# Three rounded products in place of one plain fp32 product for the attention output of the second block

## The reference, cut to what matters

```
def dsa_attention(q, k, v, qi, ki, wi, k_sel):          # block of 128 queries
    ...                                                  # the 128 best keys of each query are chosen
    s = jnp.einsum('bqgrd,bqkgd->bqgrk', qg, kg) * scale
    s = jnp.where(valid[:, :, None, None, :], s, -jnp.inf)
    p = jax.nn.softmax(s, axis=-1)
    o = jnp.einsum('bqgrk,bqkgd->bqgrd', p, vg)          # the product that is changed
```

## Time and profile before

| | us |
|---|---|
| median of three runs | 1981.89 |
| span of the profiled execution, first to last instruction | 1979.5 |
| TensorE busy, matrix products (PE) | 1954.4 |
| TensorE busy, loads of the stationary operand (PEld) | 1586.5 |
| VectorE busy (DVE) | 1212.9 |
| ScalarE busy (ACT) | 728.8 |
| GpSimd busy (POOL) | 875.7 |

### The profile page before, as it was taken

How to read it: one execution, slowest core, us unless ns; L and a number is a source line. 1 busy time by engine, 2 the same in 40 slices (tenths; PEclk the granted TensorE clock), 3 DMA queues, 4 the chain that set the end, 5 groups by cost and what they waited for, 6 DMA issues and landing times.

```text
span 1979.5 us, 23758 instructions
## 1 busy us (share of the span) xinstructions
PE 1954.4 (99%) x9127; PEld 1586.5 (80%) x9127; DVE 1212.9 (61%) x2188; ACT 728.8 (37%) x1057; POOL 875.7 (44%) x595
## 2 busy tenths in 40 slices
PE   8999999999999999999999999999999999999999
PEld 6777888888888766888888878888888888787787
DVE  3455442499999774222223588888888874795344
ACT  4345432232333344222223333333333334635452
POOL 1000000006878888887700677777787600720000
DMA  7543333146666667866657799999999923332122
GB/s 245 169 136 121 124 111 127 43 142 146 147 147 144 139 118 199 244 146 146 148 183 253 249 373 355 381 373 349 363 375 359 387 75 96 86 88 62 44 95 85
DMA packets 178592, 374.91 MB, mean 189 GB/s; under 512 B 56880, under 2 KB 92208, under 8 KB 169008
## 3 DMA queue, kind: packets, MB, share of 16 engines
q1 hardware_dynamic: 109264, 277.03, 41.0%
q0 software_dynamic: 64000, 84.12, 16.5%
q10 hardware_dynamic: 5216, 12.26, 1.7%
HBM read 312.38 MB, written 60.95 MB: 189 GB/s over the span
## 4 chain that ended last, share of the span: by engine, by line
PE 95%; DVE 3%; ACT 1%; issue 1%; DMA 0%; SPq 0%; DVEq 0%; ACTq 0%
PE bank L1558 35%; PE bank L329 18%; PE bank L331 17%; PE bank L330 17%; PE bank L1438 1%; PE bank L2237 1%; PE bank L1184 1%; PE bank L2217 1%; PE bank L548 1%; PE bank L2226 1%; PE bank L569 0%; DVE mix L919 0%; PE bank L419 0%; DVE v_low L1813 0%; PE bank L604 0%
## 5 line engine op out<-in xcount | busy, mean ns | idle before, releaser
L1412 POOL DMA_INDIRECT gates_scratch<-slot_gate,slot_place x256 | 441.5, 1725 | 299.4 <-DVE slot_place L1379 205.6
L1558 PE MATMUL bank<-xn_low,u_high 128*128 128x512 f32 x1024 | 410.3, 401 | 0.0
L1558 PE MATMUL bank<-xn_high,u_high 128*128 128x512 f32 x1024 | 399.9, 391 | 0.0
L1558 PE MATMUL bank<-xn_high,u_low 128*128 128x512 f32 x1024 | 398.6, 389 | 0.0
L1609 DVE TENSOR_TENSOR u_low<-u_raw,u_high 128x1024 fp32r<-128x1024 f32 x128 | 156.4, 1223 | 265.1 <-ACT u_high L1580 264.7
L329 PE MATMUL bank<-v_high,w_high 128*128 128x512 f32 x768 | 299.3, 390 | 1.4 <-DVE v_low L1813 1.4
L330 PE MATMUL bank<-v_low,w_high 128*128 128x512 f32 x768 | 299.1, 390 | 0.0
L331 PE MATMUL bank<-v_high,w_low 128*128 128x512 f32 x768 | 299.1, 389 | 0.0
L322 DVE TENSOR_TENSOR weights_low<-weights_raw,weights_high 128x1024 fp32r<-128x1024 f32 (+1 forms) x105 | 127.7, 1217 | 228.2 <-ACT weights_high L311 228.2
L1704 POOL DMA_INDIRECT row_unit<-units_scratch,slot_place x128 | 175.1, 1368 | 145.8 <-DMA units_scratch<-hidden 107.1
L1697 POOL DMA_INDIRECT row<-in_peer_v,row_places x128 | 188.7, 1474 | 82.4 <-DVE x L1824 48.9
(11 more groups left out here) (344 smaller groups left out, 3046.7 us busy)
## 6 DMA issues: line engine op xcount, KB each, us to landing
u_raw<-in_peer_u SPq DMA_DIRECT2D x128, 512.0 KB, 4.1
v_raw<-in_peer_v SPq DMA_DIRECT2D x64, 1024.0 KB, 7.6
weights_raw<-in_w_in SPq DMA_DIRECT2D x62, 512.0 KB, 3.6
hidden_scratch<-hidden SPq DMA_DIRECT2D x128, 192.0 KB
hidden_in<-hidden_scratch SPq DMA_DIRECT2D x32, 768.0 KB, 11.7
gates_scratch<-nothing POOLq DMA_DIRECT2D x32, 512.0 KB, 2.9
gate_in<-gates_scratch SPq DMA_DIRECT2D x32, 512.0 KB, 7.3
weights_raw<-in_w_out SPq DMA_DIRECT2D x16, 512.0 KB, 3.7
```

Source lines behind the costliest of these rows:

```text
L1412: pool.engine.indirect_dma_start(gates, bass.IndirectOffsetOnAxis(p.slot_place[t][:, i:i + 1], 0), p.slot_gate[t][:, i:i + 1], None, compu ...
L1558: step = pe.engine.matmul(m.bank[b][:, :], left[:, k, :], right[:, k, :], start=(done == 0), stop=(done == 3 * KT - 1))
```

## The change

The transposed weights and the values are each kept as a rounded part and a rest, and their product is `three_products` (240 records) instead of one plain fp32 product per block (160 records). The rounded part of the weights is what ScalarE's copy writes (now fp32r); the rest is a new subtraction on VectorE for each item, `apply`, which reads bank 6 and the rounded part. Bank 6 is now free, and the product may start, when that subtraction is done (`a_split`), no longer when the copy is done (`a_copied`). VectorE takes the subtraction of item i-1 after the bias of item i and before the bias of item i+1. The values are split once: one more ScalarE copy and one more VectorE subtraction of 128x512 in `keys_and_index`. Four new tiles are in places that were free at that time. The semaphore `keys_twice` is called `kv_copied` and counts one more; an unused semaphore is gone.

```diff
     def apply(i):                                   # TensorE
...
-        m.bank_freed[6] = (s.a_copied, i + 1)
+        m.bank_freed[6] = (s.a_split, i + 1)
     def multiply(i):
...
-        pe.wait_ge(s.a_copied, i + 1)
+        pe.wait_ge(s.a_split, i + 1)
...
         for j in range(t + 1):
-            step = pe.engine.matmul(m.bank[7][:, head * HEAD_DIM:(head + 1) * HEAD_DIM], w.turned_weights[i % 2][:, j * P:j * P + P],
-                                    w.kv[:, j, P + group * HEAD_DIM:P + (group + 1) * HEAD_DIM], start=(j == 0), stop=(j == t))
+            step = three_products(pe.engine, m.bank[7][:, head * HEAD_DIM:(head + 1) * HEAD_DIM],
+                                  (w.turned_high[i % 2][:, j, :], w.turned_low[i % 2][:, j, :]),
+                                  (w.value_high[:, j, part], w.value_low[:, j, part]), j == 0, j == t)
@@ ScalarE, keys_and_index
             move(TURN_KEYS + g, w.keys[:, g, :])
             yield 0.1
+        act.engine.activation(w.value_high[:, :, :], w.kv[:, :, P:2 * P], ACT.Copy).then_inc(s.kv_copied, 1)
@@ ScalarE, apply
-        act.engine.activation(w.turned_weights[i % 2][:, 0:n], m.bank[6][:, 0:n], ACT.Copy).then_inc(s.a_copied, 1)
+        act.engine.activation(w.turned_high[i % 2][:, 0:t + 1, :], m.bank[6][:, 0:n].rearrange("p (j q) -> p j q", q=P), ACT.Copy).then_inc(s.a_copied, 1)
@@ VectorE, keys_and_index
+        dve.wait_ge(s.kv_copied, 5)
+        dve.step(v.tensor_tensor(w.value_low[:, :, :], w.kv[:, :, P:2 * P], w.value_high[:, :, :].bitcast(F32), ALU.subtract))
         dve.wait_ge(s.kiw_moved, TT)
         rotate(3, w.kiw[:, :, 0:IDX_DIM], 1, 4, 8)
@@ VectorE
+    def apply(i):
+        t, head = A_ITEMS[i]
+        n = (t + 1) * P
+        dve.wait_ge(s.a_copied, i + 1)
+        if i == 0:
+            dve.settle()
+        if i >= 2:
+            dve.wait_ge(s.a_multiplied, i - 1)
+        v.tensor_tensor(w.turned_low[i % 2][:, 0:t + 1, :], m.bank[6][:, 0:n].rearrange("p (j q) -> p j q", q=P),
+                        w.turned_high[i % 2][:, 0:t + 1, :].bitcast(F32), ALU.subtract).then_inc(s.a_split, 1)
...
-    attending = attention_pieces(prepare(), choosing, chosen, score, lambda i: None, multiply)
+    attending = attention_pieces(prepare(), choosing, chosen, score, apply, multiply)
```

More of the change, by code:

```diff
@@ L82, in __init__ @@
     def __init__(self, nc):
-        self.tensor_step, self.scalar_step, self.vector_step, self.pool_step = semaphores(
-            nc, "tensor_step scalar_step vector_step pool_step")
+        self.scalar_step, self.vector_step, self.pool_step, self.a_split = semaphores(
+            nc, "scalar_step vector_step pool_step a_split")
         self.tables_arrived, self.lambda_arrived, self.subln_arrived, self.alibi_arrived, self.decay_arrived = semaphores(
@@ L137, in __init__ @@
             nc, "tables_two_arrived rotary_arrived rotary_reduced rotary_ready gains_ready last_squared gained_squared")
-        (self.made, self.kiw_moved, self.heads_squared, self.rotated, self.keys_twice, self.index_four, self.two_turned, self.two_moved, self.index_weight) = semaphores(
-            nc, "made kiw_moved heads_squared rotated keys_twice index_four "
+        (self.made, self.kiw_moved, self.heads_squared, self.rotated, self.kv_copied, self.index_four, self.two_turned, self.two_moved, self.index_weight) = semaphores(
+            nc, "made kiw_moved heads_squared rotated kv_copied index_four "
                 "two_turned two_moved index_weight")
@@ L206, in __init__ @@
         self.s = s = Signals(nc)
-        self.pe = Lane(nc.tensor, s.tensor_step)
+        self.pe = Lane(nc.tensor, None)
         self.act = Lane(nc.scalar, s.scalar_step)
@@ L1934, in __init__ @@
         self.keys = rows.tensor("keys", [P, KV_HEADS, T], F32)
-        rows.at += KV_HEADS * T * 4
+        self.value_high = rows.tensor("value_high", [P, TT, P], F32R)
+        self.value_low = rows.tensor("value_low", [P, TT, P], F32R)
         self.q = rows.tensor("q", [P, TT, T], F32)
@@ L1954, in __init__ @@
         turned_region, weights_region = Region(nc, turned_at), Region(nc, final_gain_at)
-        self.turned_weights = [turned_region.tensor(f"turned{i}", [P, T], F32) for i in range(2)]
+        self.turned_high = [turned_region.tensor(f"turned_high{i}", [P, TT, P], F32R) for i in range(2)]
+        over_kv = Region(nc, p.scores_at + 8192).tensor("turned_low", [P, TT, 2 * P], F32R)
+        self.turned_low = [over_kv[:, :, i * P:(i + 1) * P] for i in range(2)]
         assert turned_region.at <= keep.stream_at
@@ L2161, in keys_and_index @@
         for g in range(KV_HEADS):
-            pe.wait_ge(s.keys_twice, 4)
+            pe.wait_ge(s.kv_copied, 4)
             turn_out(TURN_KEYS + g, lambda t: w.keys_twice[:, t, 2 * g:2 * g + 2, :].rearrange("p a d -> p (a d)"))
```

3 lines of the change are left out of this document (2 added, 1 removed).

## The result

The changed kernel takes 2004.18 us (median of four, 2002.69 to 2005.39), the kernel before beside it 1982.12 (1981.25 to 1982.58). The ratio is 1.0112 (95% interval 1.0100 to 1.0124), +22.1 us. The prediction was +15.2 with a range up to 2003.5: the direction was right, the size 7 us too small, and the time lies just above the range. The profiled execution has a span of 2002.9 us against 1979.5.

The account below looks back on a forecast made before the run. TensorE, busy 1954.4 of 1979.5 us, was taken to bound the kernel. Records 8.4, waits 6.6 and values 0.2 sum to 15.2 us, which on 1981.9 gives 1997.1 us; range 1990.0 to 2003.5.

Parts of the forecast that it names:

- Records: 8.4 forecast: Attention products on TensorE: 240 rounded records replace 160 plain ones at 0.105 us each, 25.2 against 16.8, costing 8.4 us.
- the hidden part of the longer products: Before TensorE's transpositions: the longer product standing between two of them hides 0.105 us of wait for each block.
- Waits: 6.6 forecast: TensorE's transpositions at eight tight items and the last product wait for VectorE's subtraction: 6.6 us together, bounds 0 to 17.2.
- Values: 0.2 forecast: Key stage: VectorE's subtraction for the values stands ahead of `rotate(3)` and delays a transposition by 0.2 us, bounds 0 and 0.7.
- Hidden waits: Rival: in the attention TensorE pays for its records and up to 2 us of waits; 1991 us, chance 0.17.
- both rivals with a faster record: Attention products: rounded records at the pace of columns, 1980.6 us, or of the fp16 load, 1986.0 us; chance 0.03 each.
- The chain that binds at every item: Rival: each of the 32 subtractions is in TensorE's way in the attention, +26.3 us, 2008.2 us; chance 0.11.
- T(8), T(14) and T(26) wait: Sign: the transpositions of items 8, 14 and 26 wait for VectorE by 1 to 2 us each.
- Idle time ahead of transpositions and small products: Sign: TensorE's idle time before its transpositions and small products goes up by 5 to 9 us.
- The stretch 15 us longer: Sign: first score to last product takes 15 us longer, and everything behind it lasts as before.

Follow-up runs that it names:

- records_only: Changed kernel, but the third record reads the rounded weights again, no rest subtraction is made, and bank 6 is free at ScalarE's copy; 1989.6 us, ratio 1.0036.
- filled: Changed kernel plus 4, 16, 4 and 7 unread 64-column products on TensorE ahead of its waits at items 11, 14, 18 and 26; 2000.5 us, ratio 1.0089.
- filled_thin: Changed kernel plus 4, 16, 4 and 7 unread products of 2 columns on TensorE ahead of items 11, 14, 18 and 26; 2005.6 us, one run.

## Where the prediction was right, and where it was wrong

The +21.85 us of aligned span come apart like this, each from two runs:

- records: `records_only` less its loss to the clock, 8.5 - 1.7 = 6.8;
- waits: from T(0) to T(31) `filled` takes 91.30 and `records_only` 82.55, both at clock 1.00 there: 8.75, and some 0.25 ahead of the last product;
- clock: the changed kernel takes 97.11 there and `filled` 91.30: 5.8;
- not placed: 0.25.

*Records: 8.4 forecast, 6.8 measured.* The distance was nearly right (0.111 against 0.105), and that columns don't set it, too. The 0.105 is a mean over seven distances of which the first is 0.06 and the other six are 0.111, so a plain record in a row keeps the same pace as a rounded one. The prediction counted the hidden part of the longer products under the waits; the records alone show it on their side.

*Waits: 6.6 forecast, 9.0 measured.* By item, from the same two runs: item 8 0.79 (0.9 forecast), item 14 1.92 (1.8), 10 and 11 together 1.20 (0.9), 18 1.25 (0.9), 25 and 26 together 1.79 (0.95), 22, 28 and 31 together 1.72 (0.85). The mechanism holds at each, but at the end of a tile it reaches one step further back than I priced. The rows at items 24 to 26 of the changed kernel, and two of the kernel before:

```profile
1861.18 0.62 PE L2229 MATMUL bank<-ident,weights 128*128 128x128 f32 x4
1861.66 0.72 ACT L2442 ACTIVATE weights<-weights,small_two 128x512 f32<-128x512 f32 x1 [1.23 <-DVE small_two L2755]
1863.45 1.23 DVE L322 TENSOR_TENSOR weights_low<-weights_raw,weights_high 128x1024 fp32r<-128x1024 f32 x1 [1.83 <-ACT weights_high L311]
1864.60 0.68 DVE L2766 TENSOR_TENSOR turned_low<-bank,turned_high 128x512 fp32r<-128x512 f32 x1
1866.17 0.19 PEld L329 LDWEIGHTS bank<-value_high,turned_high 128*128 128x128 f32 x1 [0.35 <-DVE q L2778]
1866.76 0.68 DVE L2755 CUSTOM_DVE_ANT_0 weights<-bank,bias 128x512 f32<-128x512 f32 x1
1869.30 0.69 DVE L2766 TENSOR_TENSOR turned_low<-bank,turned_high 128x512 fp32r<-128x512 f32 x1 [1.85 <-ACT turned_high L2450]
1870.14 0.63 PE L2229 MATMUL bank<-ident,weights 128*128 128x128 f32 x4 [0.96 <-DVE turned_low L2766]
```

```profile
1845.94 0.60 PE L2226 MATMUL bank<-ident,weights 128*128 128x128 f32 x4
1847.21 1.23 DVE L322 TENSOR_TENSOR weights_low<-weights_raw,weights_high 128x1024 fp32r<-128x1024 f32 x1 [2.30 <-ACT weights_high L311]
```

From L322 to the transpositions of item 26 it is 5.36 us before and 6.69 after: the 1.33 are the two subtractions of 0.69 that I priced. But L322 itself stands 2.27 us behind the transpositions of item 24 instead of 1.27. The bias of item 25 now comes behind the subtraction of item 23, the exponential of item 25 waits for that bias, ScalarE's rounded part of the weights (L311) stands behind the exponential, and L322 waits for it. So three subtractions are in the way there and not two. TensorE's wait of 0.35 for `q` adds nothing: it lies inside the time in which this chain is still on its way to item 26. Whether items 11 and 18 are longer than forecast by the same step I did not follow.

Records and waits together: 15.0 forecast, 15.8 measured. The overlap of the two was put in different places, but their sum was sized well.

*Values: 0.2 forecast, 0.07 measured.*

*The step that failed* is the one that isn't in the sum. The prediction took every term at the full clock, because the profile of before shows 1.00 throughout, and asked only how long TensorE would stand, not what it would do behind it. It stood for 2.00 us at item 14 and for 0.96 at item 26, and behind both the granted clock fell to 0.50, for 10.2 and 3.4 us. That is 5.8 of the missing 6.65 us (21.85 - 15.2); `filled` shows it by giving that much back up to T(31) with the same waits. The rest of the miss is in records and waits together, 0.8, and what isn't placed. The Trainium skill has the rule that I should have weighed (TensorE: Matmul & The Clock Gate, Part 1: The HAM clock gate): a monitor passes the full clock or half of it by how busy TensorE has lately been. The traces agree that there are just two levels, 1.00 and 0.50.

*The rivals.* Hidden waits are out (0.79 us at item 8 and 1.92 at item 14 were paid). So are both rivals with a faster record. The chain that binds at every item (2008.2) lies 4 us above what was measured, and it isn't the mechanism: in 21 of the 31 intervals `filled` and `records_only` differ by less than 0.2 us.

*What would show it.* Records 0.111 apart and loads of 0.19: right. T(8), T(14) and T(26) wait: 1.71, 2.00 and 0.96, the last just under the 1 us foretold. Idle time ahead of transpositions and small products up by 5 to 9 us: 1.3 before, 7.3 + 0.6 + 0.2 now, 6.8 more: right. The stretch 15 us longer: it was 20.7 from T(0) to T(31), and this is the line that showed the error. From the start of the last record of 64 columns to the end both kernels take 111.4 us, so nothing is passed on.

## What to carry over

When a change makes TensorE wait in pieces of a microsecond or two where it had run through, ask what its clock will be behind the waits: here 13.7 us at half clock came with 7.3 us of waiting. It is a risk and not a rule: the same wait brought a fall in one execution and none in the next, so carry it as a chance with its price, and look at the mean clock of every run and not of one trace. Such waits can be bought off with products that nobody reads, or better by moving the work that they wait for ahead in its queue; compare distances item by item, since the total hides whether waits or clock were gained. A product of few columns is priced in records, each with its load: whether 2 or 64 columns follow and whether they are rounded made no difference, a third record did. And when a piece of work is added to a queue in strict order, follow the chain back to the last point where that queue ran ahead: at item 26 it was one subtraction more than priced.

## What the runs showed of the hardware that was not expected

- The granted clock fell to 0.50 with no wait at all ahead of it in `records_only`, behind 4.8 us of nothing but 64-column products and transpositions at the end of the attention, with TensorE 100% busy.
- Whether the clock falls is not the same from one execution to the next. Near the start of the program, where all kernels are alike, TensorE waits 2.08 us for VectorE, up to 87.5 to 88.0 us, in all thirteen profiled executions; behind it the clock fell to 0.50 for 3.4 us in seven and not in the other six. With the same wait of 1.71 us at item 8, it fell in `filled_thin` and not in the changed kernel and `filled`. The lengths at half clock in the attention were 3.4, 6.8 and 10.2 us. What decides is open.
- Rounded records of 64 columns, two per block, ran at the pace of plain fp32 (0.43 us less in 76), and 16 records of 2 columns took 1.93 us.
- The start of the attention lay at 1789.5 to 1789.8 us in five of the profiled executions and at 1791.1 to 1791.8 in the other eight: seven by that fall, the changed kernel by the wait at 1521 us. It must be taken out before single executions are compared at a microsecond.
